# Two-block transformer on one core: head norms moved into the q/k/v products, state-space tables moved to GpSimd, opening reordered

## What is computed

```
def memory_cross_attention(h, mem_n, w_q, w_kv, q_gain, k_gain, w_o):
    q = rms_norm_2((h @ w_q).reshape(b, t, MEM_HEADS, MEM_HEAD_DIM), q_gain)     # 4 heads of 256
    k, v = jnp.split(mem_n @ w_kv, 2, axis=-1)
    k = rms_norm_2(k.reshape(b, m, MEM_HEADS, MEM_HEAD_DIM), k_gain)
    p = jax.nn.softmax(jnp.einsum('bthd,bmhd->bhtm', q, k) * MEM_HEAD_DIM ** -0.5, axis=-1)
    ...
for l in range(DEPTH):                       # 2 layers
    ... mixing: l = 0 time mix + s5_ssm, l = 1 diff_attention (q, k normed over 16 groups of 64)
    y_mem = memory_cross_attention(rms_norm_2(h, norm_xattn[l]), rms_norm_2(mem, norm_mem[l]), ...)
    ... l = 0: swiglu, l = 1: mixture of experts
```

## Time and profile before

| | us |
|---|---|
| three timed runs | 2926.44, 2943.56 (median), 2945.67 |
| the profiled execution | 2930.94 |
| its span, first to last instruction | 2929.1 |
| TensorE busy | 2601.7 (89%), 13581 matmuls |
| VectorE busy | 1915.5 (65%) |
| ScalarE busy | 1515.6 (52%) |
| GpSimd busy | 90.4 (3%) |
| mean granted clock of TensorE | 0.937 of full speed |

### The profile page before, as it was taken

One profiled execution on the slowest core, in us unless ns is written; L12 is line 12 of the kernel. 1 busy time (PEld: TensorE's weight loads), 2 busy tenths in 40 slices (PEclk: granted clock), 3 DMA queues, 4 the chain that ended last, 5 costly groups with the idle time before them and its releaser, 6 DMA issues. The chain is left out here.

```text
span 2929.1 us, 37611 instructions
## 1 busy us (share of the span) xinstructions
PE 2601.7 (89%) x13581; PEld 2117.6 (72%) x13582; DVE 1915.5 (65%) x2368; ACT 1515.6 (52%) x1875; POOL 90.4 (3%) x115
## 2 busy tenths in 40 slices
PE   6889887997869698998978879998998999999998
PEld 5678765776765486887757657777887777777777
DVE  4555545796668544555455459885454889888888
ACT  3544335443221343444444347774443777777776
POOL 0000011000143000000100000000000000000000
PEclk9999988998887898999989879999998999999999
DMA  8346512455200541464414239995554899999996
GB/s 276 133 153 191 164 58 94 144 179 164 68 2 1 201 158 58 159 198 147 144 40 147 72 115 365 327 361 188 183 182 152 313 319 348 330 357 330 358 328 225
DMA packets 333583, 566.24 MB, mean 193 GB/s; under 512 B 21929, under 2 KB 126712, under 8 KB 333080
## 3 DMA queue, kind: packets, MB, share of 16 engines
q1 hardware_dynamic: 333464, 564.59, 56.9%
HBM read 561.19 MB, written 6.50 MB: 194 GB/s over the span
## 5 line engine op out<-in xcount | busy, mean ns | idle before, releaser
L1240 DVE TENSOR_TENSOR weights_split<-ring,weights_split 128x1024 fp32r<-128x1024 f32 x676 | 819.3, 1224 | 266.5 <-ACT weights_split L1235 229.2
L1315 PE MATMUL ps<-weights_split,expert_split 128*128 128x512 f32 x3864 | 914.6, 394 | 25.9 <-DVE expert_split L1411 17.7
L1235 ACT ACTIVATE weights_split<-ring 128x1024 fp32r<-128x1024 f32 x676 | 715.3, 1061 | 353.1 <-PE ps L1315 341.8
L1315 PEld LDWEIGHTS ps<-weights_split,expert_split 128*128 128x128 f32 x3864 | 722.3, 189 | 193.2 <-DVE weights_split L1240 38.2
L289 DVE TENSOR_TENSOR weights_split<-ring,weights_split 128x2048 fp32r<-128x2048 f32 x182 | 413.4, 2272 | 418.0 <-ACT weights_split L280 417.4
L280 ACT ACTIVATE weights_split<-ring 128x2048 fp32r<-128x2048 f32 x182 | 345.0, 1896 | 436.4 <-PE ps L460 259.0
L459 PE MATMUL ps<-normed_split,weights_split 128*128 128x512 f32 x1248 | 446.4, 400 | 25.5 <-PEq L342 25.1
L460 PE MATMUL ps<-normed_split,weights_split 128*128 128x256 f32 x1248 | 353.7, 283 | 0.0
L459 PEld LDWEIGHTS ps<-normed_split,weights_split 128*128 128x128 f32 x1248 | 239.6, 192 | 82.1 <-issue 27.5
L365 PE MATMUL ps<-weights_split,hidden_split 128*128 128x512 f32 x1032 | 244.4, 393 | 17.4 <-DVE weights_split L289 9.3
L460 PEld LDWEIGHTS ps<-normed_split,weights_split 128*128 128x128 f32 x1248 | 239.9, 192 | 1.4
(11 more groups left out here) (393 smaller groups left out, 2339.0 us busy)
## 6 DMA issues: line engine op xcount, KB each, us to landing
ring<-moe_w_gate SPq DMA_DIRECT2D x112, 1024.0 KB, 5.2
ring<-moe_w_up SPq DMA_DIRECT2D x112, 1024.0 KB, 5.3
ring<-moe_w_down SPq DMA_DIRECT2D x112, 1024.0 KB, 5.2
ring<-mlp_w_up SPq DMA_DIRECT2D x32, 1024.0 KB, 5.5
ring<-mlp_w_down SPq DMA_DIRECT2D x32, 1024.0 KB, 5.0
ring<-xa_w_kv SPq DMA_DIRECT2D x16, 1024.0 KB, 5.2
ring<-moba_w_qkv SPq DMA_DIRECT2D x12, 1024.0 KB, 12.2
ring<-da_w_qkv SPq DMA_DIRECT2D x12, 1024.0 KB, 5.2
```

The source lines that it names most:

```text
L1235: nc.scalar.activation(split_piece(p, 0), ring_piece(p), ACT.Copy).then_inc(high.sem, 1)
L1240: nc.vector.tensor_tensor(split_piece(p, 1), ring_piece(p), split_piece(p, 0).bitcast(F32), ALU.subtract)\
L1315: last = nc.tensor.matmul(ps[:, banks[half][tt], :], stationary(s, k, tt), split_piece(p, i)[:, kk * NW:(kk + 1) * NW], start=(opens and n ...
```

## The change

1. **Opening.** SP issues the first norm's gain row and the bias table right behind the constants, then two tiles, the other 14 rows and the four tiles that fill the ring. TensorE turns the gain row alone, then x; the other parameters are turned at the end of the stage (`pe_last`, `dve_last`). The second tile is split behind the normed activations.
2. **Norms over heads in the products.** `qkv_normed` takes the place of `qkv_products` and `grouped_norm` in both cross attentions and the difference attention (the first attention keeps `qkv_products`). For the cross attentions it also norms the memory, whose transposes TensorE makes behind unit 0; the stage in which SP waited is gone. The sums over heads are taken one unit late, the spreads five. The inverse is split in two halves and spread by one float32r matmul.
3. **Tables on GpSimd.** `tables_pool` has the whole chain of doublings, from the first turn on; VectorE keeps angles, first turn and coefficients.
4. **Splitting ahead.** The sparse attention's stage ends with the high and low halves of the next projection's first two tiles.

The core of the diff:

```diff
@@ norm_stage
         if ahead:
-            core.hi(e, core.taken + WS_BUFS)
+            core.hi(e, core.taken + (1 if opening else WS_BUFS))
...
+        if opening:
+            core.hi(e, core.taken + WS_BUFS)
@@ cross_attention
-    def sp(e):
-        e.wait_ge(*mem_landed.at(0))
-    stage(core, sp=sp)
...
-        norm_stage(core, mem, MS, at_col("norm_mem_2", 8 * layer), 0)
-        qkv_products(core, core.XS, MS, qk, vN, None)
-    gpe, gact, gdve = grouped_norm(core, qk, 16, MD, "norm_xattn", gain, SCR)
-    stage(core, pe=gpe, act=gact, dve=gdve)
+        qkv_normed(core, 1, gain, qk, vN, (mem, MS, mem_gain, mem_landed))
@@ new
+def qkv_normed(core, per_unit, gain, qk, vN, memory=None, lead=None, pool=None):
...
+    def pe(e):
+        def pick(u):
...
+            if one:
+                e.wait_ge(*halves_added.at(u + 1))
+                first = u % 4 + 1
+                last = nc.tensor.matmul(ps[0:R, SUMS, cols], c("pick_all")[:, PICK - first:PICK - first + R],
+                                        both[:, u % 2, :], start=(u % 4 == 0), stop=(u % 4 == 3))
+            else:
+                e.wait_ge(*squares.at(u + 1))
...
+        for u in range(8):
+            w = core.weights(e, t0 + u)
...
+            core.fill(last, bank=True, tile=True)
...
+            if u >= 1:
+                pick(u - 1)
+            if u >= 5:
+                spread_unit(u - 5)
+        for i in range(4):
...
+            if i == 0:
+                pick(7)
+                spread_unit(3)
...
+    def act(e):
...
+        for i in range(12):
+            core.hi(e, min(t0 + i + 1 + WS_BUFS, t0 + 13))
+            if i < 8:
+                core.wait_bank(e, i)
...
+                    .then_inc(*low_kept.up())
+                e.wait_ge(*freed.at(i + 1))
...
+                nc.scalar.activation(sq[:, i % 2, :], flat(qk[:, 2 * i:2 * i + 2, :]), ACT.Square).then_inc(*squares.up())
...
+            if i == 4:
+                e.wait_ge(*sums.at(4))
+                nc.scalar.activation(root, ps[0:R, SUMS, 0:T], ACT.Sqrt, bias=eps(E_EPS256 if one else E_EPS64, R))\
+                    .then_inc(*roots.up())
...
+    def dve(e):
...
+        for i in range(12):
+            core.lo(e, min(t0 + i + 1 + WS_BUFS, t0 + 13))
+            if one and 1 <= i <= 8:
+                u = i - 1
+                e.wait_ge(*squares.at(u + 1))
...
+                V.tensor_tensor(both[:, u % 2, :], sq[:, u % 2, 0:T], sq[:, u % 2, T:2 * T], ALU.add)\
+                    .then_inc(*halves_added.up())
+            if i < 8:
+                e.wait_ge(*low_kept.at(i + 1))
+                V.tensor_tensor(qk[:, 2 * i:2 * i + 2, :], ps[:, 2 * (i % 2):2 * (i % 2) + 2, 0:T], two(low[:, i % 2, :]),
+                                ALU.add).then_inc(*freed.up())
...
+            if i in (4, 8):
+                invert(i // 4 - 1)
+            if 5 <= i <= 9:
+                apply(i - 5)
@@ S5
+    def tables_pool(self, e):
...
+        e.wait_ge(*self.turn_made.at(1))
...
+        for level in self.LEVELS:
+            count = min(ST, 512 // level)
+            for first in range(0, ST, count):
...
+                tt(x1, COS[:, :, 0:level], qc, ALU.mult)
+                tt(x2, SIN[:, :, 0:level], qs, ALU.mult)
+                tt(COS[:, :, level:2 * level], x1, x2, ALU.subtract)
+                tt(x1, COS[:, :, 0:level], qs, ALU.mult)
+                tt(x2, SIN[:, :, 0:level], qc, ALU.mult)
+                tt(SIN[:, :, level:2 * level], x1, x2, ALU.add)
@@ Opening.sp
             e.dma_start(core.const[:, :], consts).then_inc(*self.const_landed.up(16))
+            e.wait_ge(*self.rows_cleared.at(1))
+            e.dma_start(*loads[0][0]).then_inc(*self.gain_landed.up(16))
+            e.dma_start(relb[:, :], w["rel_bias"]).then_inc(*self.rows_landed.up(16))
             core.held_from = WS_BUFS
             core.issue(e, WS_BUFS)
...
+            core.held_from = 10 ** 9
+            core.issue(e, RING)
             e.wait_ge(*extd.at(1))
@@ the sparse attention's stage, ends of act and dve
+        core.hi(e, core.taken + 3 + WS_BUFS)
...
+        core.lo(e, core.taken + 3 + WS_BUFS)
```

More of the change, by code:

```diff
@@ L562, in dve @@
             add_to_x(core, e, ups * n, 4)
-        stage(core, pe=pe, act=act, dve=dve, uses=len(order))
+        stage(core, pe=pe, act=act, dve=dve, pool=beside.tables_pool if beside else None, uses=len(order))
 def project(core, srcT):
@@ L662, in pe @@
                     last.then_inc(*turned.up())
+        if opening:
+            opening.pe_last(e)
     stage(core, sp=extra_sp, pe=pe, act=act, dve=dve)
@@ L990, in gain, with mem_gain @@
         return core.cols[:, which, r + j % 2:r + j % 2 + 1]
-    gpe, gact, gdve = grouped_norm(core, qk, 16, MD, "norm_xattn", gain, SCR)
-    stage(core, pe=gpe, act=gact, dve=gdve)
+    def mem_gain(k):
+        which, r = at_col("norm_mem_2", 8 * layer + k)
+        return core.cols[:, which, r:r + 1]
+    with core.scoped("memory_split", [P, 2, KD, T], F32R) as MS:
+        qkv_normed(core, 1, gain, qk, vN, (mem, MS, mem_gain, mem_landed))
     q, k = qk[:, 0:8, :], qk[:, 8:16, :]
@@ L2193, in __init__ @@
         sig = lambda n: Signal(core.nc, f"s5_{n}")
+        self.qt = [a(6528 + ST * i, ST) for i in range(2)]
+        self.turn_made = sig("first_turn")
         (self.saved, self.loaded, self.landed, self.ex, self.ang, self.trig, self.made, self.turned, self.kept_turned) = map(
@@ L2334, in first_turn @@
         tt(e, co, sh, sh, ALU.mult)
-        ts(e, co, co, -2.0, 1.0, ALU.mult, ALU.add)
+        self.core.nc.vector.tensor_scalar(co, co, -2.0, 1.0, ALU.mult, ALU.add).then_inc(*self.turn_made.up())
+        e.wait_ge(*self.turn_made.at(1))
     def coefficients(self, e):
@@ L2382, in prepare @@
             last.then_inc(*self.made.up())
-    def double(self, e, n, first, count, parts=(0, 1)):
-        tt = self.tt
-        q = self.turns
-        which = slice(first, first + count)
-        x1, x2 = (t[:, 0:count * n].rearrange("p (s n) -> p s n", n=n) for t in self.tmp)
-        qc, qs = bc(q[0][:, which], 2, n), bc(q[1][:, which], 2, n)
-        COS, SIN = self.COS[:, which, :], self.SIN[:, which, :]
-        if 0 in parts:
-            tt(e, x1, COS[:, :, 0:n], qc, ALU.mult)
-            tt(e, x2, SIN[:, :, 0:n], qs, ALU.mult)
-            tt(e, COS[:, :, n:2 * n], x1, x2, ALU.subtract)
-        if 1 in parts:
-            tt(e, x1, COS[:, :, 0:n], qs, ALU.mult)
-            tt(e, x2, SIN[:, :, 0:n], qc, ALU.mult)
-            tt(e, SIN[:, :, n:2 * n], x1, x2, ALU.add)
-        if 1 in parts and n < self.LEVELS[-1] and first + count == ST:
-            q2 = (self.qc, self.qs) if q[0] is not self.qc else (self.qc2, self.qs2)
-            tt(e, self.t1, q[0], q[0], ALU.mult)
-            tt(e, self.t2, q[1], q[1], ALU.mult)
-            tt(e, q2[0], self.t1, self.t2, ALU.subtract)
-            tt(e, self.t1, q[0], q[1], ALU.mult)
-            self.ts(e, q2[1], self.t1, 2.0, None, ALU.mult)
-            self.turns = q2
     def scan_project(self, e, p):
@@ L2973, in dve @@
-    def dve(e):
-        for i in range(2):
-            nc.vector.tensor_tensor_reduce(out=products_[:, i * 64:(i + 1) * 64], in0=lam_sb[:, 2 * i, :],
-                                           in1=lam_sb[:, 2 * i + 1, :], scale=1.0, scalar=0.0, op0=ALU.mult,
-                                           op1=ALU.add, accum_out=small[:, 80 + i:81 + i]).then_inc(*lam_sums.up())
-        e.wait_ge(*lam_exp.at(1))
-        link(e, "dve", nc.vector.tensor_tensor(small[:, 84:85], small[:, 83:84], small[:, 82:83], ALU.subtract))
-        nc.vector.tensor_scalar(lam_neg, small[:, 84:85], -LAMBDA_INIT, None, ALU.add)
-        ndve(e)
@@ L2983, in act, with dve @@
-    def act(e):
-        e.wait_ge(*lam_sums.at(2))
-        nc.scalar.activation(small[:, 82:84], small[:, 80:82], ACT.Exp).then_inc(*lam_exp.up())
-        nact(e)
-    stage(core, sp=sp, pe=npe, act=act, dve=dve, pool=pool)
+    products_ = a(9728, 2 * 64)
+    class Lambda:
+        def dve(self, e):
+            for i in range(2):
+                nc.vector.tensor_tensor_reduce(out=products_[:, i * 64:(i + 1) * 64], in0=lam_sb[:, 2 * i, :],
+                                               in1=lam_sb[:, 2 * i + 1, :], scale=1.0, scalar=0.0, op0=ALU.mult,
+                                               op1=ALU.add, accum_out=small[:, 80 + i:81 + i]).then_inc(*lam_sums.up())
+            e.wait_ge(*lam_exp.at(1))
+            link(e, "dve", nc.vector.tensor_tensor(small[:, 84:85], small[:, 83:84], small[:, 82:83], ALU.subtract))
+            nc.vector.tensor_scalar(lam_neg, small[:, 84:85], -LAMBDA_INIT, None, ALU.add)
+        def act(self, e):
+            e.wait_ge(*lam_sums.at(2))
+            nc.scalar.activation(small[:, 82:84], small[:, 80:82], ACT.Exp).then_inc(*lam_exp.up())
```

242 lines of the change are left out of this document (205 added, 37 removed).

## The result

The changed kernel takes 2971.6 us (median of 4 runs, 2969.0 to 2972.57) against 2942.56 us for the kernel before (4 runs beside it, 2926.44 to 2945.67): ratio 1.0109, 95% interval 1.0077 to 1.0141. It is 29 us slower, as forecast (+27.8 by the sum, 2964 stated). The agreement flatters the sum. Profile against profile the spans are 2970.7 and 2929.1 us, 41.6 apart, and a second profile of the kernel before has 2931.2. The sum was made from such profiles, so it was 12 to 14 us too small.

A forecast was written before the change was run, and what follows sets the result against it. TensorE, busy 89% of the span, was read as the bound. Terms 24.8 + 28.0 - 14.1 - 3.0 - 4.0 - 0.4 - 3.5 = +27.8 us on 2930.94 gave 2958.7, raised toward the timed median to 2964; range 2928 to 2992.

The forecast's parts named there:

- The ring: Cross attention products: TensorE's sum waits for VectorE's addition, behind low half, high half and TensorE's unit; eight waits of 4.9 us.
- The clock: Cross attention products: TensorE's clock falls around each standstill, costing 1.5 us each, 12.0 us per cross attention.
- Difference attention: Its products take over the norms over heads, 26.5 us removed and 12.4 added, no wait at the sums: net -14.1 us.
- Attention behind dense products: All three attentions start behind dense products instead of a low-clock stretch: about -1 us each, -3.0 together.
- Tables: Second feed-forward: state-space tables move to GpSimd, which takes turns with VectorE: -4 us, between -12.7 and +6.
- Opening: Start of the kernel: gain row comes third, so the first product starts near 26 us: -3.5 us, bounds -1 and -7.
- Splitting ahead: Sparse attention's stage: -4.9 us at the second projection's wait, +4.5 at the end of the stage before: net -0.4 us.
- The addition comes in time: Rival, cross attentions: TensorE's sum does not wait for the split; about 2862 us, half hidden 2913; chance 0.10 for both.
- GpSimd ends last: Rival, end of the second feed-forward: GpSimd finishes last, +6 and up to +12 us; about 2974 to 2980; chance 0.13.
- whole units at 1.2 GHz: Rival, cross attentions: the whole unit after each standstill runs at half speed, up to 64 us more, 3028; chance 0.06.

The follow-up runs named there:

- the addition ahead of the low half: Changed kernel, but in the cross attentions VectorE adds the two halves of the squares before making the next weight tile's low half: 2879.07 us, ratio 0.9797.
- the addition in the same turn: As the addition ahead of the low half, but VectorE adds the squares' halves right behind the unit's own addition: 2868.48 us, ratio 0.9758.
- TensorE kept busy: Changed kernel with 18 unread matmuls of 512 columns on TensorE ahead of each of the 16 waits for the addition of the squares' halves: 2941.16 us.
- the first four experiments: Changed kernel with the addition ahead of the low half, TensorE kept busy, cross attentions as before, or tables back on VectorE: 2879.07, 2941.16, 2907.66, 2979.23 us.

## Why the prediction was right, and where its terms were off

**The ring.** Eight waits of 4.9 us per cross attention were forecast; there are eight, of 4.87 in the mean. The run with the addition ahead of the low half removes six of them, and the one with the addition in the same turn a seventh. Its working, from the order of two queues and three rows, needed no measurement of the operation itself.

**The clock.** This is the step that was mis-sized. I took 1.5 us behind each standstill, from the one gap of 3.55 us in the earlier trace rows; the run with TensorE kept busy puts it at 1.9 to 2.2. I argued that "part of the slow stretch will fall into the standstill itself", and part of it does: the mean granted clock inside the second and the third standstill (1033.67:1038.39 and 1046.87:1051.59) is 0.77 and 0.82. But what comes behind them is slow for longer than I took it to be: the next 8.41 and 8.71 us of TensorE's work have a mean clock of 0.72 and 0.71, and the first work there is the pair for the sums, at 1.03 to 1.06 us instead of 0.62. The stage that I put at 125 to 132 us took 137.8. Without loss of clock my sum for it is 69.3 + 9.2 + 39.2 = 117.7 us, and the run with TensorE kept busy has 120.25, so 2.5 us were missing there; half of them are the sums' pairs, which take 0.62 us each where I had priced 0.45. The clock then costs 17.6 us in place of my 12.0, which is 5.6 more. Over both cross attentions the two make 16 us, and 67.6 us were measured (33.5 + 34.1) where the forecast, with 2 us less for the attentions behind, has 50.8.

**Difference attention.** No wait for the squares at the sums, as forecast. The stage of about 82 us took 85.1. Its three small standstills, for the root, for the inverse and near the end, are 1.14, 2.02 and 1.10 us long, where I had 1.0, 1.5 and 0.8. -12.7 in the mean of the profiles, against -14.1 and a share of the attentions' -3.0.

**Attention behind dense products.** In the cross attentions 46.4 us each instead of 48.4 and 48.2, so -2.0 and -1.8; in the difference attention nothing that shows.

**Tables.** -6.7 against -4. Taking turns was right in kind: the instruction of GpSimd that started at 592.04 waited out the low half that ended at 594.10 and then needed 1.16 us more. The Trainium skill ("SBUF — State Buffer", section "SBUF: two separate sides") says of the port pair that VectorE and GpSimd share that whichever starts first has it for its whole instruction. The trace agrees. But GpSimd was done at 677.6 us, 125.5 after its start and 18 before the stage's last product ended (696.0); I had it end with the stage. Its undisturbed 128x512 instruction takes 1.04 us, not 1.2; in the mean, with its waits for VectorE, one takes 1.79.

**Opening.** -4.1 against -3.5, within the bounds. The queue's standstill of 4.13 us has only moved behind the two ring tiles, where it is 6.34 us long; the gain row is now ahead of it and the other rows behind. What ends the stage is SP, which needs 2.90 us to hand on the bias row:

```profile
2.73 1.14 SPq L258 DMA_DIRECT2D ring<-moba_w_qkv  x2
3.91 6.34 SPq L2853 DMA_DIRECT2D rows<-ln_mlp  x1
...
15.03 5.68 SPq L258 DMA_DIRECT2D ring<-moba_w_qkv  x4
21.11 2.90 SPq L2857 DMA_DIRECT2D bias_row<-arena  x1
```

```profile
10.35 0.25 PE L2886 MATMUL ps<-const,rows 16*128 16x16 f32 x1 [10.35 <-DMA rows<-ln_attn]
...
24.99 0.77 PE L457 MATMUL ps<-normed_split,weights_split 128*128 128x512 f32 x1 [4.78 <-PEq L340]
```

**Splitting ahead.** Forecast -0.4, measured nothing.

**The rivals.** "The addition comes in time" was given 0.10; what it would be worth I put at 2862, and the two runs that make it come in time measured 2879 (two waits per stage are left) and 2868 (one). "GpSimd ends last" was wrong, and "whole units at 1.2 GHz" too: about half a round is.

**Profiles and medians.** Terms by the traces: cross +67.6 (the attentions behind them included), difference -12.7, tables -6.7, opening -4.1, splitting 0, so +44.1, with the 4 us of the mixture +40.1; the profiles differ by 39.5 to 41.6. The timed medians differ by 29, with an interval of about 23 to 41. Over all its runs the kernel before took from 2924.19 to 2945.67 us, and its two profiled ones, 2930.94 and 2933.03, lie in the lower half. The gap between the profile and the median I had bridged by 5.3 us (half of the 12.6 to the median would have been 6.3), and this, not the sum, brought the forecast to within 8 us: that the sum's 27.8 stands so near the 29 of the medians is luck. The measured 1.09% is in the class "slower", to which I had given 0.41, and not in "within 1%", which had 0.50.

## What to carry to other kernels

When a norm or another reduction is moved into a pipelined product loop, follow its chain through every engine's queue from the end of the unit that it belongs to: what counts is not whether an engine has time for the extra instruction but what stands ahead of it, above all an instruction that itself waits for the engine that will ask. Here the same work, one place earlier in VectorE's queue, is the difference between 1% slower and 2% faster than before. Price a standstill of TensorE by its length and by the slow work behind it, and take a profiled gain of a few microseconds for real only where the stretch repeats in a second profile.

## What the runs showed of the hardware that I had not expected

A standstill of 2.8 us is enough for the clock: in the run with the addition ahead of the low half, the 6.88 us behind the first of the two waits that are left have a mean granted clock of 0.54, so nearly all of them are at 1.2 GHz. Behind the standstill of 1.79 us in the run with the addition in the same turn, the next 3.19 us are at 1.00.

```profile
1024.12:1031.00 6.88, 6.88 (x22) 5.21 (x23) 3.32 (x3) 1.37 (x3) 0.00 (x0) 0.54 0.47 146
```

The execution time of one kernel goes with its mean granted clock: among the 13 runs of the kernel before that were timed with the first four experiments, the fastest, 2924.19 us, had 0.937 and the slowest, 2944.9 us, had 0.928. And work that is thrown away can shorten a kernel: 288 matmuls that nobody reads took 30 us off the changed one.
